# The first eight modulation loads in products of 32 output partitions and 4 columns on TensorE alone, with x turned between them

## The chip, the core and the metric

The kernel runs on one core of a Trainium2 chip. A core has engines that run beside each other: TensorE (PE in the profile; its weight loads are PEld), VectorE (DVE), ScalarE (ACT), GpSimd (POOL) and SyncE (SP), which issues most of the transfers. Sixteen DMA engines bring data from HBM to SBUF. The metric is the device time of one execution in microseconds; less is better.

## What is computed

A hybrid layer (attention over selected keys, a gated recurrence, retention, a mixture of experts) is followed by a second block of feed-forward layers, a gating unit and another attention, for 256 positions of 1024 features. What matters here is the beginning: the modulation is a product of one vector with a 1024 x 6144 matrix, and the first two of its six parts shift and scale the normed x before the large product with `w_in`.

```python
mod = (jax.nn.silu(c) @ ada_w + ada_b)[:, None, :]
sh1, sc1, gt1, sh2, sc2, gt2 = jnp.split(mod, 6, axis=-1)
h = rmsnorm(x, norm1_g) * (1.0 + sc1) + sh1
(aq, ak, av, iq, ik, iw, bq, bf, bi, bg, cq, ck, cv, cg, ga, gb, gc) = split_cols(h @ w_in)
```

## The kernel before

The program is written per engine (`tensor`, `scalar`, `vector`, `gpsimd`, `sync`), and each engine's work stands in the order in which it runs. Engines wait for each other by semaphores under names such as ("h", 1) or ("ada", 2). Weights come in loads of 1 MB or 0.5 MB that SyncE issues in the order of one list, `plan`. A weight piece is split into a high half H, copied by ScalarE (L1489), and a low half L, subtracted by VectorE (L2169); a product is then three products on TensorE: H by H, H by L, L by H (`three`, L577 to L579).

The modulation matrix comes in loads (g, q): g counts groups of 512 output columns, q = 0 or 1 the upper and lower half of its 1024 rows, so a load holds 4 steps of 128 rows. Groups 0 and 1 make the shift, 2 and 3 the scale. These eight loads are the first of the list, with 256-column halves of the first `w_in` pieces between them: (0,0), x, (0,1), (2,0), (2,1), two halves, (1,0), (1,1), a half, (3,0), two halves, (3,1) and the rest.

Their product is shared between two engines. VectorE (`modulation`, L2172; called by its `ahead_to` when the load's turn in the list comes) takes the first `mine[g, q]` of the 4 steps, 2 or 3 of them: it multiplies the 128 x 512 step by one column of `cs`, silu of c, and adds to `acc[g]` (L2181 the first, L2184 the others). TensorE (`first_ada`, L682) takes the other steps, with the 128 x 128 block of the matrix as weights and the column of `cs` broadcast to 128 columns, so all 128 columns of the output are equal. `first_sum` (L694) then adds VectorE's `acc[g]` into the same bank by four products with a matrix of ones. `columns(g)` (L2906, its addition is L2910) reads every 128th column of the bank and adds the bias. `gains` (L2912) makes the scale's gain out of it. `h_raw` copies the turned x out of its bank on ScalarE (L1963), `h_high` (L1970) and `h_whole` and `h_low` (L2926, L2933) make h and its two halves for a pair of 128-row chunks, cp = 0 to 3. `turn_pair` (L643, products L652) turns two chunks of x by a diagonal matrix `n1D` that carries the norm; n1D needs the root on ScalarE (L1522), a reciprocal (L2936) and two scalings (L2939) on VectorE.

TensorE's order at the start is: the transposition of c (L1357), nine `warm` products of constants (L884), `first_ada(0, 0)`, nine more, `first_ada(0, 1)`, the sum of group 0, `first_ada(2, 0)`, a transposition of bias rows (L1366), the turns 0 and 1, `first_ada(2, 1)`, the sum of group 2, the turns 2 and 3, two more transpositions, and then `first()` (L703). That walks the first 14 pieces of `w_in`, 24 products each, and puts a block of `first_ada` behind each of the first four and the sums of groups 1 and 3 behind the second and the fifth. Pieces six and later need h of the last chunks, which needs `columns(3)`.

`blocks` (L726) belongs to a later stage, the gated recurrence: it multiplies 32-column weights into the four strips of 32 output partitions in turn, 32 columns each (L729). `slot_gates` (L994) multiplies full 128-column weights by 4 columns.

## Time and profile before

| | |
|---|---|
| time, median of 3 runs | 2096.53 us (2095.65 to 2098.03) |
| profiled execution, its own time | 2095.4 us |
| its span | 2093.6 us |
| TensorE busy | 1940.2 us (93%), 12282 products |
| VectorE busy | 1148.7 us (55%) |
| ScalarE busy | 899.1 us (43%) |
| HBM read | 500.07 MB |

The profile page sums one execution: busy times, the chain of work that ended last, the costliest groups, the transfers. The trace behind it is asked for stretches: the timeline lists instructions in order of time, merged where alike, with the idle time before them and what ended it; the slices give each engine's busy time in a stretch, the granted clock of TensorE and the busy share of the DMA engines. The profiled execution is 1.1 us below the median of the runs.

### The profile page before, as it was taken

How to read it: one execution, taken by the hardware profiler on the slowest of the kernel's cores; microseconds unless marked ns; L12 is line 12 of the kernel's file. 1: busy time of each engine (PE TensorE's matmuls, PEld its weight loads, DVE VectorE, ACT ScalarE, POOL GpSimd, SP SyncE). 2: the span in 40 equal slices, each digit the busy share in tenths (PEclk: the TensorE clock that was granted, in tenths of full speed). 3: DMA queues.
4: the chain of work that ended last, by engine and by line, in shares of the span. 5: the costliest groups of instructions: out<-in, count | busy, mean ns of one | idle time of the engine just before them, and what ended most of it. 6: DMA issues, size and time to landing. Idle time of an engine off the chain costs nothing.

```text
span 2093.6 us, 29582 instructions
## 1 busy us (share of the span) xinstructions
PE 1940.2 (93%) x12282; PEld 1514.4 (72%) x12282; DVE 1148.7 (55%) x1548; ACT 899.1 (43%) x1274; POOL 113.1 (5%) x94
## 2 busy tenths in 40 slices
PE   8999999999999667666789999999999999999998
PEld 8899988889985111111148888888888888888887
DVE  6678774577663101111127666656666666666666
ACT  4555455544342000000025456545555654576454
POOL 0243121001210000000000000000000000000000
PEclk9999999999999988898899999999999999999999
DMA  9554535567987999999995755544655555525652
GB/s 377 171 164 143 181 123 170 193 227 248 312 327 311 425 422 424 423 424 423 422 399 184 239 193 181 181 161 160 202 181 181 181 181 190 178 81 166 206 181 81
DMA packets 242524, 503.43 MB, mean 240 GB/s; under 512 B 9745, under 2 KB 158898, under 8 KB 217938
## 3 DMA queue, kind: packets, MB, share of 16 engines
q1 hardware_dynamic: 241344, 500.53, 66.2%
q8 instruction: 99, 1.62, 0.3%
q10 hardware_dynamic: 898, 0.80, 0.1%
q0 software_dynamic: 144, 0.17, 0.1%
q14 instruction: 39, 0.32, 0.0%
HBM read 500.07 MB, written 1.06 MB: 239 GB/s over the span
## 4 chain that ended last, share of the span: by engine, by line
PE 73%; DMA 17%; DVE 5%; ACT 3%; issue 1%; SPq 0%; POOL 0%; ACTq 0%; DVEq 0%
PE bank L577 14%; PE bank L579 13%; PE bank L578 13%; PE bank L638 13%; DMA m<-in_expert_w_up 8%; DMA m<-in_expert_w_gate 7%; PE bank L640 7%; PE bank L1012 4%; DVE m L2169 1%; PE bank L899 1%; DMA m<-in_ffn_w_in 1%; ACT m L1489 1%; DMA m<-in_ada_w 0%; PE bank L729 0%; PE bank L649 0%
## 5 line engine op out<-in xcount | busy, mean ns | idle before, releaser
L2169 DVE TENSOR_TENSOR m<-m,m 128x1024 fp32r<-128x1024 f32 x505 | 623.4, 1248 | 289.4 <-ACT m L1489 287.4
L577 PE MATMUL bank<-m,m 128*128 128x256 f32 (+1 forms) x1960 | 661.5, 338 | 10.2 <-DVE m L2169 5.4
L579 PE MATMUL bank<-m,m 128*128 128x256 f32 (+1 forms) x1960 | 646.3, 330 | 0.0
L578 PE MATMUL bank<-m,m 128*128 128x256 f32 (+1 forms) x1960 | 646.2, 330 | 0.0
L1489 ACT ACTIVATE m<-m 128x1024 fp32r<-128x1024 f32 x505 | 524.1, 1054 | 235.9 <-PE bank L579 206.6
L638 PE MATMUL bank<-m,m 128*128 128x512 f32 x1248 | 439.8, 394 | 0.0
L577 PEld LDWEIGHTS bank<-m,m 128*128 128x128 f32 x1960 | 369.1, 188 | 57.3 <-DVE m L2169 12.2
L579 PEld LDWEIGHTS bank<-m,m 128*128 128x128 f32 x1960 | 369.1, 188 | 36.8
L578 PEld LDWEIGHTS bank<-m,m 128*128 128x128 f32 x1960 | 369.4, 188 | 35.4 <-issue 2.4
L640 PE MATMUL bank<-m,m 128*128 128x256 f32 x1248 | 352.7, 283 | 0.0
L638 PEld LDWEIGHTS bank<-m,m 128*128 128x128 f32 x1248 | 234.4, 188 | 54.0
L1012 PE MATMUL bank<-m,m 128*32 128x512 f32 x1024 | 191.7, 706 | 68.0 <-DMA m<-in_expert_w_up 45.5
L640 PEld LDWEIGHTS bank<-m,m 128*128 128x128 f32 x1248 | 234.6, 188 | 1.6
L1012 PEld LDWEIGHTS bank<-m,m 128*32 128x32 f32 x1024 | 42.3, 125 | 208.2 <-issue 85.0
L1830 ACT ACTIVATE m<-bank 128x256 f32<-128x256 f32 x156 | 59.1, 379 | 161.1 <-PE bank L640 161.1
L1023 PE MATMUL bank<-m,m 128*32 128x512 f32 x512 | 92.1, 678 | 33.7 <-DMA m<-in_expert_w_down 27.5
L2596 DVE SCALAR_TENSOR_TENSOR m<-bank,m,m 128x512 f32<-128x512 f32 x8 | 6.0, 750 | 171.2 <-PE bank L1012 171.2
L2725 DVE TENSOR_TENSOR m<-bank,m 128x256 f32<-128x256 f32 x156 | 65.7, 422 | 59.8 <-ACT m L1830 55.1
L1023 PEld LDWEIGHTS bank<-m,m 128*32 128x32 f32 x512 | 20.3, 120 | 97.5 <-DMA m<-in_expert_w_down 56.1
L2602 DVE TENSOR_TENSOR m<-bank,m 128x512 f32<-128x512 f32 x16 | 10.3, 686 | 143.3 <-PE bank L1023 143.3
L1750 ACT ACTIVATE m<-bank 128x512 f32<-128x512 f32 x8 | 4.8, 597 | 151.4 <-PE bank L1073 151.4
L1731 ACT ACTIVATE m<-m 128x512 fp32r<-128x512 f32 x16 | 9.4, 636 | 117.8 <-DVE m L2602 117.8
(361 smaller groups left out, 1432.8 us busy)
## 6 DMA issues: line engine op xcount, KB each, us to landing
m<-in_ffn_w_in SPq DMA_DIRECT2D x88, 1024.0 KB, 5.1
m<-in_expert_w_gate SPq DMA_DIRECT2D x64, 1024.0 KB, 24.2
m<-in_expert_w_up SPq DMA_DIRECT2D x64, 1024.0 KB, 23.8
m<-in_w_in SPq DMA_DIRECT2D x63, 1024.0 KB, 5.2
m<-in_expert_w_down SPq DMA_DIRECT2D x60, 1024.0 KB, 25.1
m<-in_ffn_w_out SPq DMA_DIRECT2D x44, 1024.0 KB, 4.9
m<-in_ada_w SPq DMA_DIRECT2D x24, 1024.0 KB, 5.9
m<-in_a_w_in SPq DMA_DIRECT2D x16, 1024.0 KB, 5.3
```

The source lines that it names most:

```text
L577: e.matmul(o, s[0], m[0], start=first, stop=False, skip_group_check=skip)
L578: e.matmul(o, s[0], m[1], start=False, stop=False, skip_group_check=skip)
L579: return e.matmul(o, s[1], m[0], start=False, stop=last, skip_group_check=skip)
L638: e.matmul(b[:, :].rearrange("p (h n) -> p h n", h=2), H, N.both[:, k], start=k == 0, stop=False, skip_group_check=True)
L640: ins = e.matmul(b[:, 0:256], L, N.T[0][:, k, :], start=False, stop=k == 7, skip_group_check=True)
L899: ins = e.matmul(o[k // per][:, k % per * n:k % per * n + n], xs[part][:, i, 128 * k:128 * k + 128], rv(Sx[:, i, 128 * q0:128 * q1]), star ...
L1012: ins = e.matmul(b[32 * j:32 * j + 32, :], XG[:, q, k, 32 * j:32 * j + 32], ld.raw[:, 512 * i:512 * i + 512], start=k == 0, stop=k == 7, s ...
L1023: ins = e.matmul(b[n][32 * j:32 * j + 32, :], eT[q % 2][:, 128 * c + 32 * j:128 * c + 32 * j + 32], ld.raw[:, 1024 * i + 512 * n:1024 * i ...
L1489: inc(e.activation(rv(fit(q.H, q.view.shape)), q.view, ACT.Copy), "h", skey(q, "H"))
L1830: inc(e.activation(fb[6][:, 256 * b:256 * b + 256], k[:, 256:512], ACT.Copy), "ffn", (f"f{z}c", n, c, b))
L2169: inc(e.tensor_tensor(rv(fit(q.L, q.view.shape)), q.view, fit(q.H, q.view.shape), ALU.subtract), "l", skey(q, "L"))
L2725: taken(e.tensor_tensor(o, k[:, 0:256], fb[6][:, 256 * b:256 * b + 256], ALU.add), f"f{n}{z}{c}", b, also=[(f"f{z}a", n, c, b)])
```

## The change

VectorE no longer takes part in the first eight loads: `acc` of groups 0 to 3, the table `mine` and `first_sum` go, and `modulation` is called for the later groups only. `first_ada` multiplies all 4 steps of every load. A new helper, `quads`, makes each 128 x 128 block of four products: 32 columns of the block as weights, the column of `cs` broadcast to 4 columns, and the result in one of four strips of 32 output partitions. The bank of a group is full with the last step of its second load.

At the start the nine `warm` products are replaced by `fill(0, 9)`, and the next nine by `fill(9, 16)` and `warm(2, 3)`; `fill` writes the same product over all of banks 4 to 7. Turns 0 and 1 move ahead of the bias rows and `first_ada(2, 0)`, turns 2 and 3 between the loads (2,0) and (2,1). ScalarE copies all four turns before the first H copy. VectorE's calls of `ahead_to` for the first four loads go.

```diff
-        mine = {(0, 0): 2, (0, 1): 2, (2, 0): 3, (2, 1): 2, (1, 0): 3, (1, 1): 3, (3, 0): 3, (3, 1): 3}
+            def quads(o, s, m, first=True, last=True):
+
+                for i in range(0, 128, 32):
+                    ins = e.matmul(o[i:i + 32], s[:, i:i + 32], m, start=first, stop=last, skip_group_check=True)
+                return ins
...
-                    for k in range(mine[g, q], 4):
+                    for k in range(4):
                         for i in range(4):
-                            e.matmul(b[:, 128 * i:128 * i + 128], p.view[:, k, 128 * i:128 * i + 128],
-                                     cs[:, 4 * q + k:4 * q + k + 1].to_broadcast([128, 128]),
-                                     start=q == 0 and k == mine[g, q] and i == 0, stop=False, skip_group_check=True)
-
-            def first_sum(g):
-
-                b = bank[where_is["ada", g]]
-                w.wait_ge("ada", g, 1)
-                for i in range(4):
-                    ins = e.matmul(b[:, 128 * i:128 * i + 128], acc[g][:, 128 * i:128 * i + 128], K(C_ONE), start=False,
-                                   stop=True, skip_group_check=True)
-                full(ins, "ada", g)
+                            ins = quads(b[:, 128 * i:128 * i + 4], p.view[:, k, 128 * i:128 * i + 128],
+                                        cs[:, 4 * q + k:4 * q + k + 1].to_broadcast([128, 4]),
+                                        (q, k, i) == (0, 0, 0), (q, k) == (1, 3))
+                    if q:
+                        full(ins, "ada", g)
...
-                    if n in (1, 4):
-                        first_sum({1: 1, 4: 3}[n])
...
+            def fill(lo, hi):
+
+                for j in range(lo, hi):
+                    e.matmul(bank[4 + j // 4][:, 128 * (j % 4):128 * (j % 4) + 128], K(C_ID), K(C_ONE), start=True, stop=True)
...
-            warm(9, 3)
+            fill(0, 9)
             first_ada(0, 0)
-            warm(9, 3)
+            fill(9, 16)
+            warm(2, 3)
             first_ada(0, 1)
-            first_sum(0)
-            first_ada(2, 0)
+            for cp in range(2):
+                turn_pair(("h", cp), x, 2 * cp, n1D)
             w.wait_ge("rows", 0)
             b = take("m", "rows", 0)
             full(e.transpose(b[:, 0:56], vv0[0:56, :], K(C_ID)[0:56, 0:56]), "rows", 0)
-            for cp in range(2):
+            first_ada(2, 0)
+            for cp in range(2, 4):
                 turn_pair(("h", cp), x, 2 * cp, n1D)
             first_ada(2, 1)
-            first_sum(2)
-            for cp in range(2, 4):
-                turn_pair(("h", cp), x, 2 * cp, n1D)
...
-            h_raw(0)
-            h_raw(1)
+            for cp in range(4):
+                h_raw(cp)
             ahead_to(first[0] + 1)
             h_high(0)
             h_high(1)
-            ahead_to(first[1] + 1)
-            h_raw(2)
-            h_raw(3)
             ahead_to(first[7] + 1)
...
                     if q.ada is not None:
-                        modulation(q)
+                        if q.ada[0] in acc:
+                            modulation(q)
                         continue
...
-            ahead_to(2)
             w.wait_ge("n1root")
...
-            ahead_to(3)
             b = got("rows", 0)
             taken(e.tensor_copy(VT[:, 0:56], b[:, 0:56]), "rows", 0)
             w.wait_ge("taken", ("rows", 0))
-            ahead_to(4)
             columns(0)
```

## Rows read from the trace of the kernel before

**Rows 1.** The page: its head, and the shares of the chain that ended last.

```profile
span 2093.6 us, 29582 instructions
...
PE 73%; DMA 17%; DVE 5%; ACT 3%; issue 1%; SPq 0%; POOL 0%; ACTq 0%; DVEq 0%
```

**Rows 2.** Timeline of TensorE, 11 to 24 us (start, length, line, shapes, count, idle before).

```profile
11.82 2.05 PE L690 MATMUL bank<-m,m 128*128 128x128 f32 x16 [1.12 <-DMA m<-in_ada_w]
...
15.59 0.27 PE L1366 MATMUL bank<-m,m 56*128 56x56 f32 x1
15.78 2.05 PE L652 MATMUL bank<-m,m 128*128 128x128 f32 x16
17.67 1.95 PE L690 MATMUL bank<-m,m 128*128 128x128 f32 x16
...
23.57 0.36 PE L577 MATMUL bank<-m,m 128*128 128x256 f32 x1 [0.99 <-DVE m L2933]
```

**Rows 3.** Timeline of TensorE, 25 to 49 us, inside `first()`.

```profile
25.05 0.38 PE L577 MATMUL bank<-m,m 128*128 128x256 f32 x1 [0.55 <-DVE m L2933]
...
31.06 1.05 PE L690 MATMUL bank<-m,m 128*128 128x128 f32 x8
...
32.76 0.37 PE L577 MATMUL bank<-m,m 128*128 128x256 f32 x1
...
39.47 1.05 PE L690 MATMUL bank<-m,m 128*128 128x128 f32 x8
40.27 0.36 PE L577 MATMUL bank<-m,m 128*128 128x256 f32 x1
...
47.60 0.28 PE L579 MATMUL bank<-m,m 128*128 128x256 f32 x1
48.23 0.38 PE L577 MATMUL bank<-m,m 128*128 128x256 f32 x1 [0.35 <-DVE m L2933]
```

**Rows 4.** Timeline of TensorE, 81 to 83 us and 646 to 651 us.

```profile
81.78 0.76 PE L729 MATMUL bank<-m,m 128*32 128x32 f32 x64
82.47 0.50 PE L577 MATMUL bank<-m,m 128*128 128x512 f32 x1
...
646.92 3.73 PE L994 MATMUL bank<-m,m 128*128 128x4 f32 x32
```

**Rows 5.** Timeline of ScalarE and VectorE, 11 to 21 us.

```profile
11.76 0.30 ACT L1522 ACTIVATE m<-m 128x2 f32<-128x2 f32 x1
...
13.45 0.48 DVE L2939 TENSOR_SCALAR m<-m,m 128x128 f32<-128x128 f32 x2
...
17.02 1.54 DVE L2184 SCALAR_TENSOR_TENSOR m<-m,m,m 128x512 f32<-128x512 f32 x2 [0.46 <-DMA m<-in_ada_w]
...
20.55 0.16 DVE L2910 TENSOR_TENSOR m<-bank,m 128x4 f32<-128x4 f32 x1 [1.92 <-PE bank L699]
```

**Rows 6.** Timeline of ScalarE and VectorE, 39 to 45 us.

```profile
39.69 2.01 ACT L1489 ACTIVATE m<-m 128x1024 fp32r<-128x1024 f32 x2 [1.66 <-DMA m<-in_w_in]
...
40.78 2.36 DVE L2169 TENSOR_TENSOR m<-m,m 128x1024 fp32r<-128x1024 f32 x2 [1.12 <-ACT m L1489]
44.32 0.16 DVE L2910 TENSOR_TENSOR m<-bank,m 128x4 f32<-128x4 f32 x1 [1.18 <-PE bank L699]
```

**Rows 7.** Slices (busy by engine, PEclk granted clock, DMA share, GB/s); timeline at 275 us.

```profile
22.50:25.00 2.50, 1.01 (x7) 0.77 (x6) 2.36 (x6) 2.43 (x5) 0.00 (x0) 1.00 1.06 399
275.00:280.00 5.00, 5.00 (x17) 4.09 (x18) 4.73 (x14) 0.39 (x1) 0.00 (x0) 0.66 0.64 210
650.50:660.00 9.50, 9.50 (x58) 5.50 (x58) 2.09 (x5) 1.35 (x2) 0.00 (x0) 0.82 1.01 424
...
274.97 0.50 PE L577 MATMUL bank<-m,m 128*128 128x512 f32 x1 [2.42 <-DVE m L2169]
```

**Rows 8.** Transfers: the instruction queue on the page, and an issue of the first 60 us.

```profile
q8 instruction: 99, 1.62, 0.3%
...
m<-in_consts ACTq DMA_DIRECT2D x1, 128.0 KB, 2.2
```

More of the change, by code:

```diff
@@ L398, in build @@
         vv0, vv2, vv3 = mem(24864, 128), mem(24992, 128), mem(25120, 128)
-        acc = {g: mem(o, 512) for g, o in zip((0, 1, 2, 3, 6, 7, 8, 9, 4, 5, 10, 11),
-               (51744, 31264, 52256, 31776, 36640, 36640, 35360, 35360, 43552, 43552, 44064, 44064))}
-        mine = {(0, 0): 2, (0, 1): 2, (2, 0): 3, (2, 1): 2, (1, 0): 3, (1, 1): 3, (3, 0): 3, (3, 1): 3}
+        acc = {g: mem(o, 512) for g, o in zip((6, 7, 8, 9, 4, 5, 10, 11),
+               (36640, 36640, 35360, 35360, 43552, 43552, 44064, 44064))}
         where = {0: 0, 1: 8, 3: 16, 4: 24}
@@ L2173, in modulation @@
                 g, q = p.ada
-                n = mine.get((g, q), 4)
                 w.wait_ge("ld", p.load.n)
                 w.wait_ge("cs")
-                for k in range(n):
+                for k in range(4):
                     if q == 0 and k == 0:
@@ L2185, in modulation @@
                                                      in1=acc[g], op0=ALU.mult, op1=ALU.add)
-                    inc(ins, "ada", ("adak", g, q, k), *([("ada", g, q), skey(p, "L")] if k == n - 1 else []))
+                    inc(ins, "ada", ("adak", g, q, k), *([("ada", g, q), skey(p, "L")] if k == 3 else []))
             def walk(name):
```

## The prediction

> **What bounds the kernel now.** I read the head of the page first, for the chain that ended last: 73% of it is TensorE and only 5% VectorE, and the span is 2093.6 us [rows 1]. A change to the first 48 us can therefore bring only what it moves on TensorE's own sequence there, or in a wait of that sequence. The timeline of TensorE shows that sequence. Up to 11.82 us it follows the loads: it sat idle 1.12 us before its second modulation block, until ada_w landed [rows 2]. From there to 22.3 us it runs without a pause: modulation, the turning of x, modulation, the last turn. At 23.57 the first product of `first()` starts after 0.99 us idle behind L2933, the low half of h [rows 2]. From 25.05 it is dense again until 48.23, when it has waited 0.35 us for the last L2933 [rows 3]. After 48 us nothing is edited, and what is fetched or split later is released by TensorE's progress, so I take a shift at 48 us to reach the end unchanged.
>
> **What the change removes.** VectorE loses its 17 L2184 steps and 4 first multiplications of these eight loads. They are no term of the sum, since the chain up to 48 us runs through VectorE only at L2910, L2926 and L2933. TensorE loses 44 products in `first_ada` and 16 in `first_sum`. Each call on f32 data stands in the trace as two pairs of a weight load and a multiplication: the two steps of four blocks of load (0, 1), 8 calls, are the "x16" of L690 [rows 2].
>
> **What it adds, and the price of one.** Each load now costs 4 x 4 x 4 = 64 calls, so 128 pairs; eight loads make 1024 pairs. The trace of before has the same form at L729, products of 128 rows and 32 weight columns that go to four output strips in turn, only with 32 moving columns where the new ones have 4. There 64 pairs start at 81.78 and the next product starts at 82.47 [rows 4]: 0.69 us, 10.8 ns a pair. I take this value: 128 x 10.8 ns = 1.38 us a load. Above it lies L994, 4 moving columns as well but 128 weight columns: 32 pairs in 3.73 us, 0.11 us a pair [rows 4], so 14 us a load if the strips did not overlap at all. Below it I can only say that the price isn't negative. `fill` has as many products as the `warm` calls that it replaces and is priced at nothing; it stands where TensorE waits for a load anyway.
>
> A rule of the Trainium skill speaks against my price. "TensorE: Matmul & The Clock Gate", section "Wait — 56ns, not 53.3ns?", says that the start-to-start time of products never falls below about 25 ns. By it a load would cost 3.2 us. The L729 row, at 10.8 ns, is below that floor where four strips are used, and I follow the row.
>
> **First stretch, 11.82 us to the columns of the scale.** Before: from 11.82 to 20.55, when L2910 takes the sum of load group 2 [rows 2, 5], so 8.73 us. Of these, one turn is 17.67 - 15.78 = 1.89 us and the transposition ahead of it 0.19 us [rows 2]; 6.65 us are modulation. After: both turns stand ahead of the last load, so 3 x 1.38 + 2 x 1.89 + 0.19 = 8.11 us, plus about 0.17 us until the result can be read: 20.1 us. Gain **0.45 us**. Do the moved turns wait for anything? They need n1D. The root on ScalarE ends at 12.06, and VectorE is no longer held by ada_w, so the reciprocal and the two scalings of 0.48 us [rows 5] end near 12.9, ahead of 13.2, when the second load's products end. The fourth load is there by 17.02 [rows 5], and its products start at 18.6. On ScalarE, `h_raw(2)` and `h_raw(3)` move ahead of the first H copy, which would then end at 20.3 rather than 19.5; it is needed after `h_whole(0)`, at 21.1. If that slack were gone, its 0.6 us copies would cost what they overrun. From L2910 on the chain of gains, h and L2169 keeps its order, so `first()` starts at 23.1 and gets its second part of h at 24.6 instead of 25.05.
>
> **Second stretch, inside `first()`.** Four blocks of one step and two sums go; by steps 40.27 - 39.47 = 0.80 us for one block and 32.76 - 31.06 = 1.70 us for a block and a sum [rows 3]. The other two blocks and the other sum lie alike, so all six make 0.80 x 4 + 1.70 = 4.90 us. Four loads at 1.38 us are 5.53 us. **Loss 0.63 us.** VectorE is free of the multiplications in between and splits the pieces earlier, but TensorE waited for none of those splits [rows 3]. SyncE's issues keep their order: the eight loads lie in slots used once, so no later load waits for their release, and the weights' loads behind them wait for splits that come earlier or as before. No queue gets a new instruction.
>
> **The wait at 48.23.** TensorE's last product before it starts at 47.60, at a step of 0.12 us, so it was ready at 47.72 and stood until h of the last chunks came [rows 3]. That chain begins at L2910 at 44.32, which waited for the sum issued behind the fifth piece, and takes 3.9 us [rows 3, 6]. Now that result is complete with the products of load (3, 1), which start at 39.47 - 0.45 + 3 x 0.58 - 0.90 = 39.9 and end at 41.2 [rows 3]. What is late next is VectorE's two splits at 40.78 to 43.15 [rows 6]; they stand ahead of `columns(3)` and depend on ScalarE's copies, which waited for w_in to land at 39.69 [rows 6]. So L2910 moves to 43.2 and h is ready at 47.1. TensorE gets there at 47.72 - 0.45 + 0.63 = 47.90, without a wait. It resumes at 47.90 instead of 48.23: **net gain 0.33 us** with the clock unchanged. This also bounds any gain: however cheap the new products are, h is not ready before 47.1, so no more than 1.1 us can be won.
>
> **The clock.** The new products keep TensorE's sequencer busy, but stream almost nothing. L994's 3.73 us of 4-column products ended near 650.6 [rows 4], and in the 9.5 us that follow the mean granted clock is 0.82 [rows 7]; at two levels, 2.4 and 1.2 GHz, that is 9.5 x 0.18 x 2 = 3.4 us at the lower. The same came behind an idle 2.42 us: 0.66 over 5 us from 275, again 3.4 us [rows 7]. Before, the gaps between 22.5 and 25.0 us left the clock at 1.00, with 1.01 us of work in them [rows 7]. After, a block of 1.38 us of 4-column products stands right ahead of the same gaps, and another such block follows an idle 1.5 us at 11.8. A fall costs at most half of 3.4 us where TensorE is dense, 1.7 us, and nothing in its idle parts. I take one fall near 22 to 25 us, partly in the gap, as half of that: **0.8 us**. Bounds: none, and two full ones, 3.4 us.
>
> **Sum.** The profiled execution took 2095.4 us, 1.8 beyond its span. The edits make -0.33 + 0.8 = +0.47 us, 2095.9 against it. The median of the three runs is 1.1 us above the profiled one, so I forecast 2096.53 + 0.5 = 2097.0 us, which is no change.
>
> **The rivals.**
> 1. One fall of the clock, as above: 2097.0 us, chance 0.42.
> 2. The clock holds. Nothing fell in the gaps at 22.5 [rows 7]. Then 2096.5 - 0.3 = 2096.2, with the bound of 1.1 us at 2095.4. Chance 0.27.
> 3. Two falls at their full price: 2096.5 - 0.3 + 3.4 = 2099.6, chance 0.17. Against it: the first block behind a pause is followed by dense turns.
> 4. Slower: 128 pairs in a row don't keep the rate of a burst of 64, because their instructions don't arrive. 99 instruction packets bring 1.62 MB for 12282 pairs [rows 8], so 16 KB holds the loads and products of 124 pairs, about one new block, used up in 1.38 us while the data loads fill the DMA engines. If each block had to wait for one such packet, priced by the 2.2 us of the 128 KB of constants issued beside the first loads [rows 8], a load would cost 2.2 us. The first is hidden by the wait at 11.82; seven at 0.82 us more make 5.7, so 2096.5 - 0.3 + 5.7 = 2101.9. The point from which it decides: 4.2 + 0.3 = 4.5 us over 7 x 128 pairs is 5.0 ns a pair, so from 16 ns a pair on the kernel is measurably slower. Against it stands that packets are fetched ahead of a stretch that used one packet in some 15 us until now (124 pairs at 0.12 us). Chance 0.06.
> 5. Slower: short products have a floor that the strips don't lift in a long row. It would lie between 10.8 and 112 ns a pair [rows 4]; their geometric mean, 35 ns, gives 7 x 128 x 24 ns = 21.7 us more, 2117.9. Against it: L729 shows no such floor over 64 pairs. Chance 0.03. By the 25 ns of the skill's page named above, the seven blocks would take 12.7 us more, 2108.9.
> 6. The strips don't run beside each other at all, so the change doesn't do what it says: 0.11 us a pair, 7 x (14 - 1.4) = 88 us more, 2184 us. Chance 0.01.
> 7. Something outside this reckoning gives over 4.2 us back, for instance another order of waits between 76 and 150 us. The bound of 1.1 us speaks against it. Chance 0.04.
>
> **Numbers.** A measurement of this kernel tells about 0.2%, 4.2 us, from no change. Rivals 1 to 3 lie within it (0.86), 4, 5 and 6 are slower (0.10), 7 is faster (0.04). The range goes from rival 2's bound less the 0.9 us by which the lowest run lies under the median, 2094.5, to rival 3 with the same margin, 2100.5; it leaves out 4 to 7 and little else.
>
> **What would show it.** The stretch of one new load on TensorE lasts 1.4 us; 2.2 us shows rival 4, more shows 5. L2910 of group 2 at 20.1, the first product of `first()` at 23.1. `columns(3)` near 43.2, not 44.3. No idle time before the product near 47.9. In the slices, a granted clock under 1.00 between 12 and 28 us tells rivals 1 and 3 from 2. I would be wrong if the price of a pair at 4 moving columns differs from that at 32, or if a later stage takes up the shift.

## Result and the profile after

Times are medians of the slowest core, in us, and the kernel before was timed again beside the kernel after.

| | before | after |
|---|---|---|
| median (lowest to highest) | 2096.09 (2094.23 to 2098.03), 4 runs | 2112.82 (2110.78 to 2114.32), 4 runs |
| profiled execution, its span | 2095.4, 2093.6 | 2114.32, 2112.5 |
| mean granted clock | 0.975 | 0.969 |

The ratio is 1.0078 [1.0066, 1.009]: slower by 16.7 us, outside the range of 2094.5 to 2100.5. In the code of after, the new products stand at L574 and the products of `first()` at L582 to L584; the turns are L657, the filling products L885, `columns` L2907, the low half of h L2930 and the splits of the weights L2167.

The page of after, its head, its queue of instructions and its chain of waits, against [rows 1, 8]:

```profile
span 2112.5 us, 31365 instructions
...
q8 instruction: 106, 1.74, 0.3%
...
PE 73%; DMA 16%; DVE 5%; ACT 3%; issue 2%; SPq 0%; POOL 0%; ACTq 0%; DVEq 0%
```

The kernel has 1783 more instructions and fetches 7 more instruction packets: 255 instructions a packet. In the chain, "issue" went from 1 to 2%. It is the only share that grew.

The timeline of TensorE (start, length, line, shapes, count; in brackets the idle time before and what ended it) shows where, against [rows 2, 3]:

```profile
7.33 1.32 PE L574 MATMUL bank<-m,m 128*32 128x4 f32 x128
8.59 1.83 PE L885 MATMUL bank<-m 128*128 128x128 f32 x14
12.43 0.65 PE L574 MATMUL bank<-m,m 128*32 128x4 f32 x57 [1.57 <-DMA m<-in_ada_w]
13.74 0.77 PE L574 MATMUL bank<-m,m 128*32 128x4 f32 x71 [0.66 <-issue]
14.44 3.64 PE L657 MATMUL bank<-m,m 128*128 128x128 f32 x16
...
18.20 0.52 PE L574 MATMUL bank<-m,m 128*32 128x4 f32 x40
19.94 0.91 PE L574 MATMUL bank<-m,m 128*32 128x4 f32 x88 [1.23 <-issue]
20.78 3.42 PE L657 MATMUL bank<-m,m 128*128 128x128 f32 x16
24.13 0.50 PE L574 MATMUL bank<-m,m 128*32 128x4 f32 x24
25.87 1.04 PE L574 MATMUL bank<-m,m 128*32 128x4 f32 x104 [1.24 <-issue]
29.99 0.55 PE L582 MATMUL bank<-m,m 128*128 128x256 f32 x1 [2.65 <-DVE m L2930]
...
33.34 0.41 PE L584 MATMUL bank<-m,m 128*128 128x256 f32 x1
33.55 0.41 PE L582 MATMUL bank<-m,m 128*128 128x256 f32 x1
...
35.31 1.22 PE L574 MATMUL bank<-m,m 128*32 128x4 f32 x125
38.39 0.27 PE L574 MATMUL bank<-m,m 128*32 128x4 f32 x3 [1.86 <-issue]
43.02 1.02 PE L574 MATMUL bank<-m,m 128*32 128x4 f32 x101
44.59 0.42 PE L574 MATMUL bank<-m,m 128*32 128x4 f32 x27 [0.56 <-issue]
47.99 1.31 PE L574 MATMUL bank<-m,m 128*32 128x4 f32 x128
52.27 0.62 PE L574 MATMUL bank<-m,m 128*32 128x4 f32 x52
55.81 1.24 PE L574 MATMUL bank<-m,m 128*32 128x4 f32 x76 [2.93 <-issue]
```

Three things are to be read here. **The price of a pair** is close to the forecast 10.8 ns: the block at 7.33 has 128 pairs and the next product starts 1.26 us later, 9.8 ns a pair. **The blocks break** at "issue", with nothing in the profile that TensorE waited for. The breaks lie at fixed numbers of pairs: 71 + 16 (a turn) + 1 (the transposition of the rows) + 40 = 128 pairs from the first resumption to the second stop, 88 + 16 + 24 = 128 from there to the third, and 3 + 24 of `first()` + 101 = 128 from the fourth to the fifth. Between the third resumption and the fourth stop, and between the fifth and the sixth, stand 255 recorded pairs each: two packets, the second of which had come in time. 128 pairs of a weight load and a product are 256 instructions, one packet. From resumption to resumption it takes 6.20 us (13.74 to 19.94), 5.93 (19.94 to 25.87) and 6.20 (38.39 to 44.59), while 128 pairs are worked off in 1.3. **The clock** is low in several places: the turn at 14.44 lasts 3.6 us for 1.9, and the products at 33.34 come every 0.21 us for 0.12.

The waits of the first 75 us (line waited on, total, times, longest) give the breaks their sum:

```profile
PE bank L574 <- issue: 8.5, 6, 2.9
```

The slices of after (busy by engine, granted clock, DMA share, GB/s), which stood at clock 1.00 before:

```profile
11.80:30.00 18.20, 11.79 (x420) 10.92 (x420) 3.87 (x12) 6.72 (x13) 0.00 (x0) 0.76 1.06 397
30.00:57.00 27.00, 21.65 (x609) 20.65 (x609) 10.15 (x15) 6.62 (x7) 0.00 (x0) 0.82 0.94 342
```

The timeline of VectorE shows how late the columns are for the first and for the last chunks, against [rows 5, 6]:

```profile
26.97 0.16 DVE L2907 TENSOR_TENSOR m<-bank,m 128x4 f32<-128x4 f32 x1 [8.25 <-PE bank L574]
...
57.10 0.16 DVE L2907 TENSOR_TENSOR m<-bank,m 128x4 f32<-128x4 f32 x1 [2.41 <-PE bank L574]
```

From the records behind these views, the ends of the instruction packets beside TensorE's resumptions (us of the span):

```
packet ends        12.4   18.5   24.5   37.0   43.2   54.5
TensorE goes on   13.74  19.94  25.87  38.39  44.59  55.81
```

All six resumptions come 1.3 to 1.4 us behind the end of a packet, whose transfer takes about 1.0 us. For the packets that end at 18.5, 24.5 and 43.2 the same records have the transfer start 3.6 to 3.8 us after TensorE resumed with the block before. So a period is 3.7 us until the transfer starts, 1.0 us of transfer and 1.4 us until TensorE goes on: 6.1 us. That fits one block held ahead and no more.

**Where the time went.** Up to the first product of `first()` TensorE lost 29.99 - 23.57 = 6.4 us: 0.6 because the second load came later, 3.1 in breaks (0.66 + 1.23 + 1.24), 3.1 because both turns ran at the low clock, 1.7 because the gap behind the last turn grew from 0.99 to 2.65 us (h, now as late as its columns, has no turn to hide behind), and -2.1 since the new products are cheaper. From there to L725, 81.8 us before and 99.6 after, it lost 11.4 more: 5.4 in breaks, some 6.2 by the low clock (2.1 behind 30 us, 1.5 behind 38, 2.6 behind 55), 0.3 for four new blocks against the 4.90 us removed, and -0.9 for two waits on h that are gone; 0.4 stay unassigned. Together the breaks are 8.5 of 17.8 us and the clock 9.3; the other terms, 3.0 us lost and 3.0 won, cancel. The 8.5 us are read from the waits; the 9.3 us are my estimate from products at double length, good to some tenths. The last 1.1 us of the 18.9 by which the spans differ arise in the expert stage, where the shift goes from 17.1 us at L1013 (653.6 us of after) to 18.7 at L1024 (691.7); I did not follow them up.

### The profile page after: what moved, and what is told of

Read it like the earlier page. It is cut to its first block, busy times and chain, and to the rows that moved or that the text cites. A ratio compares the mean times of both kernels' runs of the same rounds, so it can differ in the third digit from the quotient of the medians.

```text
span 2112.5 us, 31365 instructions
## 1 busy us (share of the span) xinstructions
PE 1951.8 (92%) x13186; PEld 1524.6 (72%) x13186; DVE 1135.5 (54%) x1527; ACT 899.4 (43%) x1274; POOL 112.9 (5%) x94
## 4 chain that ended last, share of the span: by engine, by line
PE 73%; DMA 16%; DVE 5%; ACT 3%; issue 2%; SPq 0%; POOL 0%; ACTq 0%; DVEq 0%
PE bank L582 14%; PE bank L584 14%; PE bank L583 14%; PE bank L643 13%; DMA m<-in_expert_w_up 8%; DMA m<-in_expert_w_gate 7%; PE bank L645 7%; PE bank L1013 4%; DVE m L2167 1%; DMA m<-in_ffn_w_in 1%; PE bank L900 1%; ACT m L1489 1%; DMA m<-in_ada_w 0%; PE bank L574 0%; PE bank L725 0%
## 5 line engine op out<-in xcount | busy, mean ns | idle before, releaser
L2167 DVE TENSOR_TENSOR m<-m,m 128x1024 fp32r<-128x1024 f32 x505 | 623.4, 1248 | 296.2 <-ACT m L1489 294.0
L582 PE MATMUL bank<-m,m 128*128 128x256 f32 (+1 forms) x1960 | 664.1, 339 | 10.5 <-DVE m L2167 4.8
L584 PE MATMUL bank<-m,m 128*128 128x256 f32 (+1 forms) x1960 | 649.1, 331 | 0.0
L582 PEld LDWEIGHTS bank<-m,m 128*128 128x128 f32 x1960 | 371.8, 190 | 57.5 <-DVE m L2167 13.4
L584 PEld LDWEIGHTS bank<-m,m 128*128 128x128 f32 x1960 | 371.7, 190 | 36.9
L1013 PE MATMUL bank<-m,m 128*32 128x512 f32 x1024 | 195.6, 716 | 67.2 <-DMA m<-in_expert_w_up 46.0
L1013 PEld LDWEIGHTS bank<-m,m 128*32 128x32 f32 x1024 | 43.4, 126 | 210.0 <-issue 88.2
L1024 PE MATMUL bank<-m,m 128*32 128x512 f32 x512 | 91.9, 693 | 32.0 <-DMA m<-in_expert_w_down 25.8
L1024 PEld LDWEIGHTS bank<-m,m 128*32 128x32 f32 x512 | 22.7, 123 | 92.2 <-DMA m<-in_expert_w_down 51.2
```

What stands on the lines that cost most here:

```text
L582: e.matmul(o, s[0], m[0], start=first, stop=False, skip_group_check=skip)
L584: return e.matmul(o, s[1], m[0], start=False, stop=last, skip_group_check=skip)
L1013: ins = e.matmul(b[32 * j:32 * j + 32, :], XG[:, q, k, 32 * j:32 * j + 32], ld.raw[:, 512 * i:512 * i + 512], start=k == 0, stop=k == 7, s ...
L1024: ins = e.matmul(b[n][32 * j:32 * j + 32, :], eT[q % 2][:, 128 * c + 32 * j:128 * c + 32 * j + 32], ld.raw[:, 1024 * i + 512 * n:1024 * i ...
L2167: inc(e.tensor_tensor(rv(fit(q.L, q.view.shape)), q.view, fit(q.H, q.view.shape), ALU.subtract), "l", skey(q, "L"))
```

## Experiments

Four theories were set against each other. S: TensorE's instructions come in blocks of 128 pairs, at most one in some 6.1 us while the loads fill the DMA engines. C: the clock alone. O: the new order of the turns. P: the price of a pair. Each kernel was timed beside the kernel before; a ratio is its time over that kernel's, with its 95% interval.

### The order of the turns alone

Before, with the new order of the turns and of ScalarE's copies, and nothing else.

```diff
             first_sum(0)
-            first_ada(2, 0)
+            for cp in range(2):
+                turn_pair(("h", cp), x, 2 * cp, n1D)
...
-            for cp in range(2):
+            first_ada(2, 0)
+            for cp in range(2, 4):
                 turn_pair(("h", cp), x, 2 * cp, n1D)
...
-            h_raw(0)
-            h_raw(1)
+            for cp in range(4):
+                h_raw(cp)
             ahead_to(first[0] + 1)
```

> The kernel before with only the reordering: turns 0 and 1 of x ahead of the load (2,0), turns 2 and 3 between (2,0) and (2,1), and ScalarE copying all four turns first. The split between VectorE and TensorE stays. Theory S (TensorE waits for its own instructions: a 16 KB block of them, 128 pairs, comes every 6.1 us at most while the loads fill the DMA engines) expects no change, 2095 to 2098 us, since no instruction is added. Theory C (the loss is the lower clock that follows 4-column products) expects the same. Theory O (the new order of turns and ScalarE copies delays the start) expects a good part of the loss here, 2100 us or more.

Measured: 2099.68 (10 runs), ratio 1.0016 [1.0007, 1.0026], so 3.2 us slower; S and C had both expected no change (2095 to 2098), and O 2100 or more. Its timeline of TensorE:

```profile
16.62 1.16 PE L690 MATMUL bank<-m,m 128*128 128x128 f32 x8
...
18.65 2.05 PE L652 MATMUL bank<-m,m 128*128 128x128 f32 x16 [0.87 <-DVE m L2907]
...
26.43 0.55 PE L577 MATMUL bank<-m,m 128*128 128x256 f32 x1 [2.78 <-DVE m L2930]
```

The second turn waits 0.87 us for a bank that `columns(0)` has to free. Now that both turns stand ahead of the last load, h isn't ready until 2.78 us after TensorE has run dry, for 0.99 before [rows 2]. `first()` starts 2.9 us late and its first 3 us run at the low clock (0.21 us a product). So O has a price of its own, in a kernel whose start isn't held up otherwise.

### After with the old order of the turns

```diff
-            for cp in range(2):
-                turn_pair(("h", cp), x, 2 * cp, n1D)
+            first_ada(2, 0)
...
-            first_ada(2, 0)
-            for cp in range(2, 4):
+            for cp in range(2):
                 turn_pair(("h", cp), x, 2 * cp, n1D)
             first_ada(2, 1)
+            for cp in range(2, 4):
+                turn_pair(("h", cp), x, 2 * cp, n1D)
```

> The changed kernel with the old order of TensorE's turns and of ScalarE's copies, everything else as changed. In the kernel before, the new order alone cost 3.2 us. Theory S: in the changed kernel TensorE's start is paced by its instructions, a block of 128 pairs in about 6.1 us, and the old order needs 16 pairs fewer ahead of the columns of the scale but the same blocks; it gains 0 to 2.5 us, 2110 to 2113 us. Theory O, by which the order carries its 3.2 us here as well and the products the rest: 2109 to 2110 us.

Measured: 2112.13 (4 runs), ratio 1.0078 [1.0061, 1.0095], the same as after. A row of its timeline, and one of its waits:

```profile
20.49 1.14 PE L574 MATMUL bank<-m,m 128*32 128x4 f32 x71 [4.27 <-issue]
```

```profile
PE bank L574 <- issue: 12.1, 6, 4.3
```

What the order gives back goes into longer breaks: 12.1 us for 8.5, while the clock is low for 17.1 us up to 60 us and in after for 23.9. The time alone hardly parts the 2112 of S from the 2109 to 2110 of O; the breaks do. The start of after is paced by its instructions, and the order carries nothing there. The 3.2 us of the first experiment are therefore no term of the 16.7.

### Half and three quarters of the products

After with 64 and with 96 pairs a load. Both leave out part of the modulation: the first two, the second one of every four blocks of 128 rows.

```diff
-                    for k in range(4):
+                    for k in (0, 3):
```

> The changed kernel with two of the four steps of each of the first eight loads left out (k = 1 and 2), so 64 pairs a load instead of 128; the modulation is then only part of the sum. Theory S: 512 pairs fewer are four instruction blocks fewer, the stalls inside the products (8.5 us in six pieces) shrink to 0 to 3 us and most falls of the clock go with them; 2096 to 2101 us. Theory C: blocks of 4-column products still stand ahead of the gaps, the clock falls as often, only 8 x 0.6 us of product time go: 2106 us or more.

```diff
-                    for k in range(4):
+                    for k in (0, 1, 3):
```

> The changed kernel with three of the four steps of each of the first eight loads (k = 2 left out), 96 pairs a load, between the changed kernel's 128 (2112.8 us) and the 64 that brought 2094.6 us. If the price lay in the products alone, a third step would cost 7 x 0.31 = 2.2 us: 2097 us. Theory S: 256 pairs fewer than the changed kernel are two blocks fewer of eight, stalls come back at the start and behind some pieces, with falls of the clock behind them: 2100 to 2107 us, about in the middle.

Measured: with 64 pairs 2094.56 (10 runs), ratio 0.9991 [0.9981, 1.0]; with 96 pairs 2103.15 (6 runs), ratio 1.0031 [1.0018, 1.0044]. With after that is a series of 2094.6, 2103.2 and 2112.8: about 9 us for each 256 pairs. By their price, 256 pairs cost 2.5 us. The 2094.6 lies 1.4 us below the range that S gave. With 64 pairs no break is left. With 96, in the waits:

```profile
PE bank L574 <- issue: 3.2, 2, 2.0
```

Of both timelines of TensorE, that with 64 pairs first:

```profile
18.05 0.72 PE L574 MATMUL bank<-m,m 128*32 128x4 f32 x64
22.46 0.55 PE L582 MATMUL bank<-m,m 128*128 128x256 f32 x1 [3.28 <-DVE m L2930]
```

```profile
45.51 1.24 PE L574 MATMUL bank<-m,m 128*32 128x4 f32 x76 [2.01 <-issue]
```

C had 2106 and more for 64 pairs, and by the price of the products alone 96 pairs would have cost 2.2 us; neither explains the series. Of the falls of the clock, one is left with 64 pairs. The clock is low from 21.2 to 28.0 us; the gap of 3.28 us hides only its first 1.2 us, and the first 5.6 us of `first()` run at half rate in it. Even so, the last low half of h is done 1.6 us earlier than before, and L725 comes at 80.2 us for 81.8. With half of the products left out, then, the gain is 1.9 us, with an interval that reaches no gain at all; that is near the 1.1 us that the prediction set as its bound.

### Products that nothing uses, with quiet and with busy DMA engines

Before, with 1024 pairs (128 rounds over the four strips, two pairs a call) on constants ahead of `gemm2("aq", ...)`, where hardly a transfer runs; and with 512 such pairs behind `slot_gates()` in the expert stage, where the loads fill the DMA engines.

```diff
+            b = take("m", "dummy")
+            for _ in range(128):
+                for i in range(0, 128, 32):
+                    e.matmul(b[i:i + 32, 0:4], K(C_ID)[:, i:i + 32], K(C_ONE, 4), start=True, stop=True, skip_group_check=True)
...
             gemm2("aq", hT, h_ready)
```

> The kernel before with 1024 pairs of the new form (32-column weights into four strips, 4 moving columns, of constants, result unused) in one row ahead of gemm2(aq), behind the stage where the loads fill the DMA engines. It measures the instruction supply by itself. At the 9.8 ns a pair that a whole block showed in the changed kernel it costs 10 us: about 2107 us, which is what theory C expects plus one or two falls of the clock (2109). Theory S with a supply as slow as in the loaded stage (6.1 us per 128 pairs) expects 8 x 6.1 = 49 us less two blocks in store: 2133 to 2145 us, with a stall every 128 pairs. Should the supply be slow only for the crowded DMA engines, the stalls are there at first and shrink once the loads in flight have landed: 2115 to 2125 us.

```diff
                         slot_gates()
+                        d = take(6, "dummy")
+                        for _ in range(64):
+                            for i in range(0, 128, 32):
+                                e.matmul(d[i:i + 32, 0:4], K(C_ID)[:, i:i + 32], K(C_ONE, 4), start=True, stop=True,
+                                         skip_group_check=True)
```

> The kernel before with 512 pairs of the new form, of constants and unused, behind slot_gates in the expert stage, where the expert weights keep the DMA engines full. The time says little, since that stage waits for transfers (0 to 20 us more). The period between stalls is the measurement: with quiet DMA engines (share 0.17) it was 3.7 to 4.5 us per 128 pairs, in the changed kernel's first stage (share 1.05) near 6.1. Theory S with a fetch that queues behind the data expects 5.5 to 7 us here; were the 6.1 us something of the start alone, it would be near 4 again.

Measured: the first 2126.44 (4 runs), ratio 1.014 [1.0123, 1.0157], 30 us for 1024 pairs that by 9.8 ns would be 10. That lies between the ranges given for a supply slow only beside crowded DMA engines (2115 to 2125) and for 6.1 us a block throughout (2133 to 2145). The second took 2113.02 in a single run; the period was the measurement there. Timeline and slice of the first:

```profile
123.36 1.45 PE L1395 MATMUL bank<-m 128*32 128x4 f32 x153
127.36 1.89 PE L1395 MATMUL bank<-m 128*32 128x4 f32 x128 [2.55 <-issue]
131.36 1.88 PE L1395 MATMUL bank<-m 128*32 128x4 f32 x128 [2.12 <-issue]
```

```profile
127.00:150.00 23.00, 11.31 (x768) 10.81 (x768) 4.43 (x5) 0.00 (x0) 0.90 (x1) 0.50 0.17 50
```

and of the second:

```profile
655.30 1.89 PE L1068 MATMUL bank<-m 128*32 128x4 f32 x128 [2.56 <-issue]
661.49 1.89 PE L1068 MATMUL bank<-m 128*32 128x4 f32 x128 [4.31 <-issue]
665.77 1.62 PE L1068 MATMUL bank<-m 128*32 128x4 f32 x107 [2.39 <-issue]
```

```profile
655.30:661.50 6.20, 1.89 (x130) 1.81 (x130) 0.00 (x0) 0.00 (x0) 0.00 (x0) 0.50 1.00 419
661.50:665.80 4.30, 1.91 (x132) 1.82 (x133) 0.00 (x0) 0.00 (x0) 0.00 (x0) 0.50 0.43 177
```

These products wait for no load, no bank and no engine, and yet they stop every 128 pairs. That settles S: what is short is the supply of instructions. A block comes every 4.0 us at a mean DMA share of 0.17 (127.36 to 131.36, for instance; the six periods lie between 3.7 and 4.6), after 6.19 us (655.30 to 661.49) at a share of 1.00, and after 4.28 us (661.49 to 665.77) at 0.43. So the full DMA engines account for some 2 us of the 6.1; the other 4 are there without them. The records of the packets show where: with quiet engines the transfer starts 1.1 to 2.0 us after a resumption, takes 0.9 to 1.5 us, and TensorE goes on 1.2 to 1.5 us behind its end. In the period at a share of 1.00 the start alone comes after 3.8 us, with 1.0 and 1.3 us behind it. The difference arises before the transfer starts, not in the transfer. Even at the low clock 128 pairs take but 1.89 us, so the breaks don't come from the clock.

### Other shapes of the same products

Three versions of after that compute the same in fewer, larger products: two strips of 64 weight columns (64 pairs a load); 128 weight columns with 4 moving columns, and with 128 moving columns (32 pairs a load each).

```diff
-                for i in range(0, 128, 32):
-                    ins = e.matmul(o[i:i + 32], s[:, i:i + 32], m, start=first, stop=last, skip_group_check=True)
+                for i in range(0, 128, 64):
+                    ins = e.matmul(o[i:i + 64], s[:, i:i + 64], m, start=first, stop=last, skip_group_check=True)
```

> The changed kernel with 64-column weights into two strips of 64 output partitions: 64 pairs a load instead of 128, the whole sum computed. A pair is dearer, near 30 ns by the 64-column form of the recurrence (32 pairs in 1.15 us with their tail), 1.8 us a load against 1.25. Theory S: half as many instructions, so few stalls; 7 x 0.55 = 4 us of dearer products on the path against over 8 us of stalls and some clock falls gone: 2097 to 2103 us, faster than the changed kernel. Theory C: as much 4-column work ahead of the gaps, the clock falls as often: 2110 to 2117 us.

```diff
-                for i in range(0, 128, 32):
-                    ins = e.matmul(o[i:i + 32], s[:, i:i + 32], m, start=first, stop=last, skip_group_check=True)
+                ins = e.matmul(o, s, m, start=first, stop=last, skip_group_check=True)
```

> The changed kernel with whole 128-column blocks as weights and 4 moving columns: 16 calls, 32 pairs a load instead of 128, at L994's 0.112 us a pair 3.6 us a load against 1.25. Theory S: no stalls for instructions at all, three loads and the turns before the columns of the scale, four loads in first(): 3 x 3.6 + 4.0 against 8.7 and 4 x 3.6 against 4.9, less the 0.5 us wait, +15 us, 2111 us, plus what the clock takes. Theory C: 3.6 us blocks of 4-column products let the clock fall behind nearly every one, 2 to 4 us more than with 128 moving columns: 2113 to 2116 us.

```diff
+                ins = e.matmul(o, s, m, start=first, stop=last, skip_group_check=True)
...
-                            ins = quads(b[:, 128 * i:128 * i + 4], p.view[:, k, 128 * i:128 * i + 128],
-                                        cs[:, 4 * q + k:4 * q + k + 1].to_broadcast([128, 4]),
+                            ins = quads(b[:, 128 * i:128 * i + 128], p.view[:, k, 128 * i:128 * i + 128],
+                                        cs[:, 4 * q + k:4 * q + k + 1].to_broadcast([128, 128]),
```

> As the run with 32 pairs a load, but with 128 moving columns instead of 4: same count, same weights, same price of a pair (0.112 us by L690 and L994 alike). Both theories: 2096 + 15 = 2111 us and no fall of the clock inside the blocks. The difference of the two runs is the clock's part alone: theory C expects 3 us or more between them, theory S does not need any and leaves room for 0 to 3 us.

Measured: two strips 2104.82 (4 runs), ratio 1.0047 [1.003, 1.0064]; whole weights with 4 columns 2138.77, ratio 1.0193 [1.0174, 1.0212]; with 128 columns 2111.83, ratio 1.0075 [1.0059, 1.009]. No block breaks at "issue" in any of the three. One row of two strips:

```profile
15.99 2.04 PE L574 MATMUL bank<-m,m 128*64 128x4 f32 x64
17.95 2.05 PE L657 MATMUL bank<-m,m 128*128 128x128 f32 x16
```

A block is 1.96 us, 30.6 ns a pair: half the pairs of after, but 0.7 us more a load, and still 8.0 us less in all, with no break for instructions. The time lies 1.8 us above my upper bound, but its four runs lie far apart, 2099.8 to 2108.8. The trace is of the fastest, which is inside the range: there `first()` starts in a stretch of low clock, which makes 2.6 of the 5.6 us that TensorE is late at L725. What the slower runs lost more, no trace shows. The kernels with whole weights, 4 columns first:

```profile
17.91 6.83 PE L573 MATMUL bank<-m,m 128*128 128x4 f32 x32
24.59 3.76 PE L656 MATMUL bank<-m,m 128*128 128x128 f32 x16
```

```profile
13.54 3.74 PE L573 MATMUL bank<-m,m 128*128 128x128 f32 x32
17.11 1.95 PE L656 MATMUL bank<-m,m 128*128 128x128 f32 x16
```

The version with 128 columns came out where its sum had it, at 2111. That the one with 4 columns differs from it by 27 us is a miss of all theories; I had given the clock at most 4. (One of its four runs took 2130.19, the others 2138.7 to 2139.8; so the size differs from run to run.) Per pair it takes 0.213 us for 0.117, and the turns between take 3.8 for 1.9. TensorE starts at half rate in after and in both of these kernels: the first filling products take some 0.23 us each. In after the records have it at 1.00 by 7.6 us and with 128 columns by 8.7 us; with whole weights and 4 columns it stays at half rate until 39.7 us, and falls again five times between 43 and 81 us, though TensorE's only idle time there is the gap of 2.7 us ahead of `first()`. At one clock the two shapes take the same time (3.73 us for 32 pairs with 4 columns [rows 4], 3.74 with 128); only the moving columns differ. With 128 columns the clock is low just once in the first 60 us, from 32.6 to 36.0, behind the gap ahead of `first()`. So in these kernels the long blocks of 4-column products went with a clock that stayed low or fell, and the same blocks of 128 columns did not. This is C. It doesn't follow that it works alone in after, whose blocks are about a third as long: with two strips, where as many blocks of 4 columns stand and none breaks, the clock is low once, for 6.8 us, and with 64 pairs for 6.8 us too, but in after for 23.9 us in five stretches. So most of the low clock in after came together with the breaks, not from such blocks alone. The slice of the kernel with whole weights and 4 columns at its start reads:

```profile
5.00:20.00 15.00, 15.00 (x73) 15.00 (x72) 0.65 (x3) 4.08 (x7) 0.00 (x0) 1.00 1.06 402
```

The clock stands at 1.00 there, though the durations of the rows are those of half the rate. The column shows 1.00 until the first change that was recorded, so at the start of a kernel a row's duration is the better witness.

### The same products under the old division of work

Before's division, with VectorE and TensorE in turn, and its order; only TensorE's own steps and sums become products of 32 output partitions and 4 columns, 32 pairs for 8 at a step. It also takes `fill` as after has it.

```diff
                         for i in range(4):
-                            e.matmul(b[:, 128 * i:128 * i + 128], p.view[:, k, 128 * i:128 * i + 128],
-                                     cs[:, 4 * q + k:4 * q + k + 1].to_broadcast([128, 128]),
-                                     start=q == 0 and k == mine[g, q] and i == 0, stop=False, skip_group_check=True)
+                            quads(b[:, 128 * i:128 * i + 4], p.view[:, k, 128 * i:128 * i + 128],
+                                  cs[:, 4 * q + k:4 * q + k + 1].to_broadcast([128, 4]),
+                                  q == 0 and k == mine[g, q] and i == 0, False)
```

> The kernel before with its division between VectorE and TensorE and its order kept; only TensorE's steps and the sums take the new form (32-column weights, four strips, 4 columns). 352 pairs for the steps and 128 for the sums instead of 120. Theory S: at most 96 pairs in one row, about 128 pairs in 6 to 7 us, so hardly a stall, and the cheap products count at last: the columns of the scale some 1.7 us earlier, h of the last chunks as in the run with half the steps: 2094 to 2096 us, 0.5 to 2 us below before. Theory C: the clock falls as in the changed kernel, 2099 us or more. Theory P (small products in themselves are slower than the trace of before promised) 2100 us or more.

Measured: 2093.73 (2092.66 to 2095.12, 11 runs) against 2096.16, ratio 0.9989 [0.998, 0.9998]: 2.4 us faster than before, and faster than both kernels. Its timeline:

```profile
16.23 3.78 PE L658 MATMUL bank<-m,m 128*128 128x128 f32 x16
19.94 1.19 PE L575 MATMUL bank<-m,m 128*32 128x4 f32 x96
...
24.20 0.36 PE L583 MATMUL bank<-m,m 128*128 128x256 f32 x1 [0.82 <-DVE m L2944]
```

No block breaks: at most 96 pairs stand together. One turn falls under the low clock, so `first()` starts 0.6 us later than before, and yet the last half of h is done 1.3 us earlier. Its time is 0.3 us below the range of S, and C and P, which had 2099 and 2100 or more, fall for this kernel. The cheap product pays a little, where its instructions are few enough to have been fetched; whether `fill` has a part in the 2.4 us was not run by itself.

### The same with TensorE kept busy

The last one, with 11 filling products more in the two waits ahead of that turn.

```diff
-            warm(9, 3)
+            fill(9, 16)
+            warm(8, 3)
             first_ada(0, 1)
             first_sum(0)
+            warm(5, 3)
             first_ada(2, 0)
```

> The run that kept the old division and order and took the new form (2093.7 us), with six dense products of constants (128 columns) more ahead of load (0,1) and five behind the sum of group 0, in waits of 1.8 and 1.4 us for transfers. There the clock fell to 1.2 GHz from 13.7 us on and the first turn took 3.8 us instead of 1.9. If dense products in the waits hold the clock, that turn takes 1.9 us again and first() starts 1.5 to 2 us earlier. The end should gain far less, 0 to 0.6 us (2093.1 to 2093.8), because h of the last chunks waits for the w_in load and VectorE's two splits, not for TensorE: the bound that the prediction gave. Were the bound wrong, the whole 1.5 to 2 us would arrive: 2091.7 to 2092.2 us. If the clock falls all the same, nothing changes at all.

Measured: 2094.73 (11 runs), ratio 0.9993 [0.9984, 1.0002]; I had expected 2093.1 to 2093.8, so there is no gain over its model; its own gain on before is 1.2 us, with an interval that reaches zero, so the 2.4 us of the model may be somewhat lucky.

```profile
16.23 2.05 PE L658 MATMUL bank<-m,m 128*128 128x128 f32 x16
...
20.40 3.05 PE L658 MATMUL bank<-m,m 128*128 128x128 f32 x16
```

The first turn is at full speed again, but now the second has part of a low stretch. The last half of h starts at 46.0 us, at 46.2 without the filling: either way it hangs on the weights that land at 39.7 and their splits [rows 6], as in the prediction. What TensorE wins ahead of that isn't seen at the end.

## Why the prediction was wrong, step by step

The step that failed is the term "1.38 us a load", taken for all eight loads in a row, with a slow supply of instructions left out of the sum as a rival of 0.06 and 5.7 us. In its place the traces show blocks of 128 pairs that come every 6.1 us, with 8.5 us of breaks; and for the clock, put at 0.8 us, about 9.3 us.

**Right: the price of a pair.** Forecast 10.8 ns from L729, measured 9.8 over 128 pairs in a row. The 25 ns that the Trainium skill gives in "TensorE: Matmul & The Clock Gate", section "Wait — 56ns, not 53.3ns?", are not borne out by the block at 7.33; with two strips instead of four, 30.6 ns a pair were measured. Rivals 5 and 6 fall with it; that the measured 2112.8 lies between the 2108.9 and the 2117.9 of rival 5 is chance.

**Nearly right: the bound of a gain.** I held that no more than 1.1 us can be won, since the splits of w_in come next. Two of the kernels without breaks that won had the last half of h 1.3 and 1.6 us earlier by their traces, and 2.4 and 1.9 us at the end by their ratios.

**Wrong: rival 4, by its size and its chance.** Its mechanism was there, down to the count: 16 KB, one new block. But a packet was priced at the 2.2 us of a transfer's row [rows 8]. In fact a block comes every 6.1 us with full DMA engines and every 4.0 with quiet ones, of which the packet's own transfer is 0.9 to 1.5. A row of another queue's transfer isn't the period of a queue that asks for one piece at a time. The argument against the rival was "fetched ahead": one block is, and the first load ran unbroken; the second already breaks. The point of decision, 16 ns a pair, was sound: with the breaks the eight loads took (8 x 1.26 + 8.5) / 1024 = 18.1 ns. With a period of 6.1 us the end of the loads is simple to work out: from the first resumption at 13.74 to the last product of the last load TensorE works off some 970 pairs, the turns and `first()` included, so it needs seven more packets. Seven periods make 56.4 us, where the forecast had the loads end at 41 and the trace has the last resumption at 55.8 and the end at 57. The profile of before gives no such period, since nothing in it used a packet fast enough; a rate that no row bounds deserved more than 0.06, and a wider range.

**Wrong: the clock, one fall at 0.8 us.** The records of the clock have five low stretches up to 62 us, of 3.4 us (from 14.4, 21.2 and 38.3) and 6.8 us (from 28.0 and 55.3), which cost 9.3 us by the estimate above. [Rows 7] had shown that a fall follows a block of such products; I took one since I took the blocks as islands in dense work. With the breaks they were blocks of short products with a pause in or beside them, five times; the kernels with such blocks and no breaks (two strips, 64 pairs) have one low stretch each. The bound of 3.4 us came from counting two.

**Wrong: the moved turns cost nothing.** They were checked for what they wait on (n1D) and not for the bank, nor for what they had hidden: behind the last turn h is late by 2.65 us instead of 0.99. In the kernel before this costs 3.2 us by itself; in after it was hidden by the breaks, so it isn't what made the forecast wrong.

**Point by point of what would show it.** Block of a new load 1.4 us: 1.24 and 1.26 where it isn't broken, else 1.9 to 4.7. L2910 of group 2 at 20.1: L2907 at 26.97. First product of `first()` at 23.1: 29.99. `columns(3)` near 43.2: 57.10. No idle time near 47.9: the wait on h is gone, but 2.93 us of "issue" stand at 55.8. Clock under 1.00 between 12 and 28 us: it was, with 0.76 from 11.8 to 30.0. No later stage took the shift up: 17.8 us at L725, 18.9 at the end.

Two questions stay open. Why only one block is held ahead, and what happens in the 1.1 us and more before a quiet transfer starts and in the 1.2 us and more behind its end, nothing here shows. And the breaks and the clock were not parted within after itself: the 8.5 and 9.3 us are a reading of its trace. That the breaks come from the supply is shown by the unused products. That the clock can be low beside blocks of 4 columns without breaks is shown by the whole weights; but how much of the 9.3 us would be left in after without its breaks is not shown, and the one low stretch of the kernels with two strips and with 64 pairs speaks for little of it.

## What to carry to other kernels

Where an edit swaps few long instructions for many short ones, work out how many instructions it places in how many microseconds, and set this against the rate at which their packets can arrive (here 256 instructions in 4 to 6 us), before the price of a single one is believed. A profile in which nothing uses them fast doesn't show that rate; a block of unused products measures it in one run. The number of pairs in the stretch counts, and not only the size of a group: 480 pairs in groups of 32 to 96 won 2.4 us, 768 in groups of 96 lost 7.0, and 1024 in groups of 128 lost 16.7. Ask of every moved step also what it had been hiding.

## What the runs showed of the hardware

- **TensorE's instructions** come in packets of 16 KB, 256 instructions or 128 pairs: one block every 6.1 us beside full DMA engines (share 1.00 to 1.07), every 4.0 us at a share of 0.17, as if one block were held ahead. Beside full engines the packet's transfer starts 3.6 to 3.8 us after a resumption, with quiet ones 1.1 to 2.0 us. It takes 0.9 to 1.5 us, and TensorE goes on 1.2 to 1.5 us behind its end. The Trainium skill, "Runtime: NRT & Kernel Launch", section "Instruction fetch mechanics", has the blocks of 16 KiB, and the 255 instructions a packet here agree. It also says that fetching is hidden because instructions are issued more slowly than they are filled in; with pairs at 9.8 ns it was not, in five of the kernels above (after and four experiments).
- **Products with 4 moving columns and 32 weight columns** over four strips go at 9.8 ns a pair at the high clock and 14.8 at the low (1.89 us for 128); with 64 weight columns over two strips at 30.6 ns; with 128 weight columns at 0.117 us, as with 128 moving columns.
- **The clock** stayed at the lower level to 39.7 us beside 32-pair blocks of 4-column products with 128 weight columns, though TensorE was never idle from 3.2 us on, and fell again at 53.3 us, 7 us behind its last idle time; with 128 moving columns it was at the higher level from 8.7 to 32.6 us. The medians of the two kernels are 27 us apart.
- **The column of the granted clock** reads 1.00 until its first recorded change: it did so over 15 us in which 4-column products took 0.213 us each for 0.117.
